# Hybrid encoder layer: token selection on two halves with a pairwise merge, group norm on token-major sums

## The reference

```
y = ys[0] + ys[1]
mean = jnp.mean(y, axis=-1, keepdims=True)
var = jnp.mean((y - mean) ** 2, axis=-1, keepdims=True)
y = ((y - mean) * lax.rsqrt(var + GN_EPS)).reshape(B, T, RWKV_WIDTH) * lnx_w + lnx_b
...
return ((y + bonus) * g).astype(z.dtype)
```

```
cap = CAPACITY_FACTOR * n // N_EXPERTS
aff = jax.nn.softmax((x @ w_router).astype(jnp.float32), axis=-1)
gates, idx = lax.top_k(aff.T, cap)
xe = x[idx]
```

## Time and profile before

| | us |
|---|---|
| median of 3 runs | 3022.91 (3021.03 to 3023.69) |
| the profiled execution | 3021.64, span 3019.8 |
| TensorE busy | 2716.5 (90%) |
| VectorE busy | 1978.3 (66%) |
| ScalarE busy | 1429.4 (47%) |
| GpSimd busy | 317.2 (11%) |
| mean granted TensorE clock | 0.947 of full speed |

### The profile page before, as it was taken

How to read it: one execution, slowest core, us unless ns; L and a number is a source line. 1 busy time by engine, 2 the same in 40 slices (tenths; PEclk the granted TensorE clock), 3 DMA queues, 4 the chain that set the end, 5 groups by cost and what they waited for, 6 DMA issues and landing times. The chain is left out here.

```text
span 3019.8 us, 89945 instructions
## 1 busy us (share of the span) xinstructions
PE 2716.5 (90%) x39070; PEld 2112.2 (70%) x39070; DVE 1978.3 (66%) x3171; ACT 1429.4 (47%) x2140; POOL 317.2 (11%) x260
## 2 busy tenths in 40 slices
PE   5999988987999999937917999999999999999994
PEld 3455544666999999924506777788887777788882
DVE  3344066875655655452278888888888888888882
ACT  3211156772222222231224666666666666666663
POOL 0000000002131131123100100000111000001000
PEclk8999998998999999978957999999999999999997
DMA  4114143003221121034207999999999999999984
GB/s 130 33 38 144 28 166 136 1 1 86 69 65 46 52 74 53 4 147 148 109 21 281 313 302 301 325 315 311 317 314 309 308 307 298 327 318 310 316 275 156
DMA packets 283336, 547.75 MB, mean 181 GB/s; under 512 B 13344, under 2 KB 96928, under 8 KB 283008
## 3 DMA queue, kind: packets, MB, share of 16 engines
q1 hardware_dynamic: 274160, 508.57, 49.2%
q0 software_dynamic: 8848, 34.08, 4.3%
HBM read 490.18 MB, written 52.43 MB: 180 GB/s over the span
## 5 line engine op out<-in xcount | busy, mean ns | idle before, releaser
L1658 DVE SCALAR_TENSOR_TENSOR arena<-arena 128x1024 f16<-128x1024 f32 x768 | 904.5, 1221 | 99.2 <-ACT arena L1603 98.9
L1558 PE MATMUL ps<-arena 128*128 128x160 f16 x12288 | 855.3, 233 | 4.2 <-DVE arena L1667 3.1
L1558 PEld LDWEIGHTS ps<-arena 128*128 128x128 f16 x12288 | 851.9, 98 | 7.7 <-DVE arena L1667 3.2
L1603 ACT ACTIVATE arena<-arena 128x1024 f16<-128x1024 f32 x768 | 766.7, 1050 | 150.6 <-PE ps L1583 149.3
L879 PE MATMUL ps<-arena 64*64 64x32 f32 (+2 forms) x14080 | 499.3, 224 | 22.4 <-DVEq L1044 21.3
L879 PEld LDWEIGHTS ps<-arena 64*64 64x64 f32 x14080 | 479.2, 135 | 27.9 <-DVEq L1044 21.5
L1575 PE MATMUL ps<-arena 128*128 128x512 f16 x1536 | 368.0, 392 | 0.0
L387 PE MATMUL ps<-arena 128*128 128x512 f16 (+1 forms) x1584 | 285.7, 344 | 0.7 <-ACT arena L236 0.7
L1575 PEld LDWEIGHTS ps<-arena 128*128 128x128 f16 x1536 | 143.3, 100 | 186.2 <-issue 41.8
L387 PEld LDWEIGHTS ps<-arena 128*128 128x128 f16 x1584 | 154.8, 98 | 131.9 <-ACT arena L236 1.2
L1624 ACT ACTIVATE arena<-ps 128x160 f32<-128x160 f32 x256 | 77.6, 303 | 253.1 <-PE ps L1558 252.9
(11 more groups left out here) (215 smaller groups left out, 2873.3 us busy)
## 6 DMA issues: line engine op xcount, KB each, us to landing
arena<-w_gate SPq DMA_DIRECT2D x128, 1024.0 KB, 5.7
arena<-w_up SPq DMA_DIRECT2D x128, 1024.0 KB, 6.0
arena<-w_down SPq DMA_DIRECT2D x128, 1024.0 KB, 7.0
arena<-feat SPq DMA_DIRECT2D x120, 256.0 KB, 4.7
feat<-arena SPq DMA_DIRECT2D x20, 640.0 KB, 3.0
arena<-w_in SPq DMA_DIRECT2D x21, 512.0 KB, 4.0
arena<-tokens SPq DMA_DIRECT2D x20, 512.0 KB, 3.9
feat<-arena POOLq DMA_DIRECT2D x1, 7680.0 KB, 22.8
```

The lines of the kernel that those rows point to most:

```text
L1558: ins = pe.matmul(ps[:, o:o + SLOTS], part(4 * c + 2 * w + k // 4, pw) [:, k % 4, f * P:(f + 1) * P], xT2[:, px, k], start=(k == 0 and i = ...
L1603: act.activation(split[k % SPLIT][:, q * PW:(q + 1) * PW], ring[k % RING][:, q * PW:(q + 1) * PW], ACT.Copy, scale=W_SCALE).then_inc(w_hi, 1)
L1658: v.scalar_tensor_tensor(split[k % SPLIT][:, WCH + q * PW:WCH + (q + 1) * PW], ring[k % RING][:, q * PW:(q + 1) * PW], W_SCALE, split[k % ...
```

## The change

In the group norm the sums of squares are formed with tokens on partitions: `token_var` multiplies the squares, as weights, with a two-column matrix of ones per head, so that one PSUM tile of 128x20 holds the sums of all 1280 tokens and two heads. Root and reciprocal work on these 20 columns. `spread` brings the result back to channels by products with the identity, whose weights are one column broadcast to 64. Each stage is done in place in `yacc`. The low halves of the output weights move from GpSimd to VectorE, as does the gate product of the last f, and ScalarE makes the high halves in one step. The output weights come in two transfers; the gain table, a new 128x128 matrix `flip` (the identity with reversed columns) and the router weights are loaded behind them.

```diff
         with nc.Block() as block:
             @block.sync
...
-                sp.dma_start(wo_raw, w_out.rearrange("(k p) n -> p k n", p=P)).then_inc(wo_in, 16)
-                sp.dma_start(wr, w_router.rearrange("(k p) n -> p k n", p=P)).then_inc(wo_in, 16)
-                sp.dma_start(g2n, gains[1:2, :].partition_broadcast(P)).then_inc(wo_in, 16)
+                for b in range(2):
+                    sp.dma_start(wo_raw[:, RT * b:RT * b + RT], w_out[RT * b * P:(RT * b + RT) * P]
+                                 .rearrange("(k p) n -> p k n", p=P)).then_inc(wo_in[b], 16)
                 for b in range(2):
                     sp.dma_start(x6[:, b], tokens[b * P:(b + 1) * P, :]).then_inc(x6_in[b], 16)
+                sp.dma_start(g2n, gains[1:2, :].partition_broadcast(P)).then_inc(tables_in, 16)
+                sp.dma_start(flip, c_mask[:, 2 * P + (4 + 2 * len(LEVELS)) * C:]).then_inc(tables_in, 16)
+                sp.dma_start(wr, w_router.rearrange("(k p) n -> p k n", p=P)).then_inc(tables_in, 16)
...
                 pool.wait_ge(post_in, 32)
-                for f in range(RT):
-                    for k in (2 * f, 2 * f + 1):
-                        pool.wait_ge(wo_hi, k + 1)
-                        pool.tensor_tensor(wo2[:, k, 1], wo_raw[:, k], wo2[:, k, 0], ALU.subtract).then_inc(wo_lo, 1)
+                for f in range(RT - 1):
                     pool.wait_ge(normed_ready, f + 1)
-                    pool.tensor_tensor(yacc[:, f], cen[:, f % 2], gate[:, f], ALU.mult).then_inc(post_done, 1)
+                    pool.tensor_tensor(yacc[:, f], yacc[:, f], gate[:, f], ALU.mult)
...
+                def head_sum(f):
                     if f:
                         pe.wait_ge(centred, f)
-                    head_sum(0, yacc[:, f]).then_inc(sum_psum, 1)
-                    pe.wait_ge(std_ready, 2 * f + 1)
-                    head_sum(1, csq[:, f % 2]).then_inc(var_psum, 1)
+                    for o, c in CHUNKS:
+                        ins = pe.matmul(ps[:, o:o + c], onesbd[:, :], yacc[:, f, o:o + c], start=True, stop=True)
+                    ins.then_inc(sum_psum, 1)
+
+                def token_var(f):
+                    pe.wait_ge(squared, f + 1)
+                    for t in range(NTT):
+                        o = (3 + 4 * (f % 2)) * 512 + 2 * t
+                        ins = pe.matmul(ps[:, o:o + 2], csq[:, f % 2, t * P:(t + 1) * P], head_col,
+                                        start=True, stop=True)
+                    ins.then_inc(var_psum, 1)
+
+                def spread(f):
+                    pe.wait_ge(rstd_ready, f + 1)
+                    if f:
+                        pe.wait_ge(normed_ready, f)
+                    for t in range(NTT):
+                        for h in range(2):
+                            ins = pe.matmul(ps[C * h:C * h + C, 2048 + t * P:2048 + (t + 1) * P],
+                                            rstd[:, f % 2, t, h:h + 1].broadcast_to([P, C]),
+                                            ident[:, :], start=True, stop=True)
+                    ins.then_inc(rstd_psum, 1)
+
+                head_sum(0)
+                head_sum(1)
+                token_var(0)
+                for f in range(RT):
+                    if f + 2 < RT:
+                        head_sum(f + 2)
+                    spread(f)
+                    if f + 1 < RT:
+                        token_var(f + 1)
...
+                def square(f):
                     act.wait_ge(centred, f + 1)
-                    act.activation(csq[:, f % 2], cen[:, f % 2], ACT.Square).then_inc(std_ready, 1)
+                    act.activation(csq[:, f % 2], yacc[:, f], ACT.Square).then_inc(squared, 1)
+
+                def root(f):
                     act.wait_ge(var_psum, f + 1)
                     if f >= 2:
-                        act.wait_ge(normed_ready, f - 1)
-                    act.activation(inv_s[:, f % 2], ps[:, 2048:2048 + NT], ACT.Sqrt, bias=cst[:, 1:2],
-                                   scale=1.0 / 64).then_inc(std_ready, 1)
-
...
+                        act.wait_ge(rstd_psum, f - 1)
+                    act.activation(rstd[:, f % 2].rearrange("p a b -> p (a b)"),
+                                   bank(3 + 4 * (f % 2), 2 * NTT), ACT.Sqrt, bias=cst[:, 1:2],
+                                   scale=1.0 / C).then_inc(std_ready, 1)
+
+                def weights_hi(first, end):
+                    act.wait_ge(wo_in[first // RT], 16)
+                    for k in range(first, end):
                         if k >= 2:
                             act.wait_ge(wo_lo, k - 1)
-                        act.copy(wo2[:, k, 0], wo_raw[:, k]).then_inc(wo_hi, 1)
+                        act.activation(wo2[:, k, 0], wo_raw[:, k], ACT.Copy, scale=W_SCALE).then_inc(wo_hi, 1)
...
-                    if f >= 2:
-                        v.wait_ge(post_done, f - 1)
-                    v.scalar_tensor_tensor(cen[:, f % 2], ps[:, 0:NT], -1.0 / 64, yacc[:, f],
+                    v.scalar_tensor_tensor(yacc[:, f], ps[:, 0:NT], -1.0 / C, yacc[:, f],
...
+                def invert(f):
+                    v.wait_ge(std_ready, f + 1)
+                    x = rstd[:, f % 2].rearrange("p a b -> p (a b)")
+                    v.reciprocal(x, x).then_inc(rstd_ready, 1)
+
+                def normed(f):
+                    y = yacc[:, f]
+                    v.wait_ge(rstd_psum, f + 1)
+                    v.scalar_tensor_tensor(y, y, pars[:, P_LW + f:P_LW + f + 1], ps[:, 2048:2048 + NT],
+                                           ALU.mult, ALU.mult)
+                    v.drain()
+                    if f == 0:
+                        v.wait_ge(post_in, 32)
+                    v.scalar_tensor_tensor(y, y, pars[:, P_LB + f:P_LB + f + 1], bonus[:, f],
+                                           ALU.add, ALU.add).then_inc(normed_ready, 1)
+
+                def weights_lo(first, end):
+                    for k in range(first, end):
+                        v.wait_ge(wo_hi, k + 1)
+                        v.scalar_tensor_tensor(wo2[:, k, 1], wo_raw[:, k], W_SCALE, wo2[:, k, 0],
+                                               ALU.mult, ALU.subtract).then_inc(wo_lo, 1)
...
                 centre(0)
-                v.wait_ge(post_in, 32)
-                for f in range(RT):
-                    if f + 1 < RT:
-                        centre(f + 1)
-                    v.wait_ge(std_ready, 2 * f + 2)
-                    v.reciprocal(inv_s[:, f % 2], inv_s[:, f % 2])
-                    v.drain()
-                    v.scalar_tensor_tensor(cen[:, f % 2], cen[:, f % 2], pars[:, P_LW + f:P_LW + f + 1],
-                                           inv_s[:, f % 2], ALU.mult, ALU.mult)
-                    v.drain()
-                    v.scalar_tensor_tensor(cen[:, f % 2], cen[:, f % 2], pars[:, P_LB + f:P_LB + f + 1],
-                                           bonus[:, f], ALU.add, ALU.add).then_inc(normed_ready, 1)
+                centre(1)
+                invert(0)
+                centre(2)
+                normed(0)
+                invert(1)
+                centre(3)
+                normed(1)
+                weights_lo(0, 2)
+                invert(2)
+                normed(2)
+                invert(3)
+                weights_lo(2, 4)
+                normed(3)
+                v.drain()
+                v.tensor_tensor(yacc[:, RT - 1], yacc[:, RT - 1], gate[:, RT - 1], ALU.mult)
+                weights_lo(4, KD)
```

```diff
                 for t in range(NTT):
-                    if t >= 2:
-                        pe.wait_ge(affT_read, t - 1)
-                    pe.transpose(ps[0:NE, (t % 2) * 512:(t % 2) * 512 + P], logit[:, t], ident[:, :]).then_inc(affT_psum, 1)
+                    rows = slice(32 * (t // 4), 32 * (t // 4) + NE)
+                    ins = pe.matmul(ps[rows, (t % 4) * P:(t % 4 + 1) * P], logit[:, t], ident[:, :],
+                                    start=True, stop=True)
+                    if t % 4 == 3 or t == NTT - 1:
+                        ins.then_inc(affT_psum, 1)
...
-                for t in range(NTT):
-                    act.wait_ge(affT_psum, t + 1)
-                    act.copy(aff[:, t * P:(t + 1) * P],
-                             ps[0:NE, (t % 2) * 512:(t % 2) * 512 + P]).then_inc(affT_read, 1)
+                for g, n in enumerate((HALF, HALF, T1)):
+                    act.wait_ge(affT_psum, g + 1)
+                    act.copy(aff[32 * g:32 * g + NE, 0:n], ps[32 * g:32 * g + NE, 0:n])
...
+                v.memset(aff, -1.0)
+                v.memset(first_row, 0.0)
+                v.drain()
+                v.memset(first_row[32:32 + NE], float(HALF))
+                v.memset(first_row[64:64 + NE], float(T0))
...
-                    pe.transpose(ps[:, n * 512:n * 512 + NE], src[:, 0:CAP0], ident[0:NE, 0:NE])
-                    ins = pe.transpose(ps[0:CAP1, n * 512 + NE:n * 512 + 2 * NE], src[:, CAP0:SLOTS],
```

(37 more changed lines are left out.)

71 lines of the change are left out of this document (41 added, 30 removed).

## The result

The changed kernel takes 2968.28 us (median of 4 runs, 2965.15 to 2971.12), the kernel before on the same chip 3023.3 (3021.03 to 3025.28): ratio 0.9818, 95% interval [0.9801, 0.9835]. The profiled execution took 2968.59 us, 53.1 under that of before.

What follows compares the result with a forecast made beforehand. VectorE's serial rounds bound selection; group norm, far from any engine's limit, spends 32.6 of VectorE's 50.6 us on four reciprocals. Selection -29.6, transposes +1.3, group norm -31.3 make -59.6: 3021.6 to 2962.0 us, 8-in-10 range 2949 to 2984.

Steps and rivals of the forecast that it cites:

- Selection: Stage of maximum, index and replacement rounds on VectorE: 31.1 us less in rounds, 1.5 more on the way out, net -29.6 us.
- The line through two row lengths: Selection rounds on 512-token rows, interpolated between 256 and 1024 tokens: 2.395 us a round, 1.53 for the last.
- The way out: Selection, from the cast to GpSimd's gather: 1.83 us before, forecast 1.5 us longer, bounds 0.8 and 4.
- Transposes: Routing probabilities between group norm and selection: 3.8 us before, 5.0 after, forecast +1.3 us, bounds -0.7 and +4.8.
- The pass with 16 weight columns: One of 20 TensorE passes transposing the routing probabilities, at the lower clock level: taken as 0.22 us.
- Group norm: Stage where the four wide reciprocals go: forecast 52.5 us long instead of 83.8, -31.3 us.
- wait 12: Group norm: VectorE's waits after the first normalized tile, mainly for the spread, taken as 12 us from 9 to 24.
- so 0.2 to 1.6 us; I leave it inside the 12: Group norm: cost of two GpSimd products beside two-SBUF-input VectorE operations, counted within VectorE's 12 us of waits.
- an overlap of 0.27 us: A normalization beside the end of a 2.12 us GpSimd operation: 1.36 us where its like takes 1.28.
- the 1.55 that I held against the rival: Length in us that the overlapped normalization would have had if GpSimd made VectorE wait wholly; argument against the rival.
- GpSimd's gate product stops VectorE outright: Group norm rival: weight halves behind two products each wait one out, 2 x 2.88 us, in all 2968; chance 0.10.
- The other rivals: TensorE's lower clock bounds group norm, 2980, 0.16; selection per-operation cost, 2987, 0.03; weight-load waits from 0.33 us a pass, 3033, 0.03.

## Why the prediction was right, and where it was wrong

**Selection,** -29.6 forecast, -28.7 measured. The line through two row lengths held: 2.420 us a round for 2.395, the last 1.59 for 1.53, and 80 partitions cost, by that line, no more than 16. The way out was under-sized: +2.0 for +1.5, inside its bounds.

**Transposes,** +1.3 forecast, -0.1 measured. The pass with 16 weight columns took 2.72/20 = 0.136 us at the granted clock of 0.50, not 0.22: what I held for the price of the upper level with 128 columns is the price of the lower with 16. (The sum in the forecast gives +1.2, not +1.3.)

**Group norm,** -31.3 forecast, -32.1 measured, but by two errors that cancel. The spread cost 0.06 us a pass as forecast (2.40 for 40). The first tile was normalized 18.5 us after the first sum, forecast 17.5. From there VectorE was to work 23.0 us and wait 12. It was busy 27.2 and waited 6.6 of the 33.8 us up to GpSimd's first cast in the next stage.

**The failed step** is "so 0.2 to 1.6 us; I leave it inside the 12", the price of GpSimd's products beside VectorE's operations. It was 5.4 us of VectorE's time, half of it on the stage; most of the rest stood where VectorE would have waited for the spread, so the two errors are not independent. I had read the price from an overlap of 0.27 us, in which the one had nearly ended when the other began: such a row can hardly tell a slower operation from one that stands until the other is done. The halves that stood ended 1.1 us behind the product's end, where one alone takes 1.22, so some 0.1 us of an overlap costs nothing. By that estimate the row should have shown about 1.4 us, not the 1.55 that I held against the rival; it showed 1.36. My rival "GpSimd's gate product stops VectorE outright" was right as a mechanism: two pairs, 2.7 us each for its 2.88. The rule that I named there, the Trainium skill, "SBUF — State Buffer", section "SBUF: two separate sides", holds here, and the row that I set against it was too short to speak against it. That the rival's 2968 is also the measured time is chance: the group norm ended where the forecast had it, since VectorE waited less than I took: TensorE was at its upper level until the 6.10 us pause, and the lengthened pairs filled some of its waits, which come to 9.0 us without the products.

**The rest.** From 2962.0 to the profiled 2968.6 are 6.6 us. The change's own stages gave 1.3 more than forecast; 4.6 came from the spread up to the norm, 5.3 from the experts, where TensorE's wait behind VectorE's code fetch is 3.9; the projection, the gap ahead of the first maximum and the final norm came out 2.5 shorter together than the forecast had them, and the execution lies 2.3 us above its span instead of 1.8. The other rivals fell: TensorE's clock bounded no round for long, and no pass came near 0.33 us (the worst spread 4.53/40 = 0.11).

## What to carry to other kernels

Before work is laid on GpSimd to spare VectorE, look at what VectorE runs beside it: where both take two operands from SBUF, the product cost VectorE almost its full length (2.7 of 2.9 us), and doing it on VectorE in 1.5 us was cheaper (group norm 46.3 for 48.2). Put the small operation that another engine waits for ahead of the long ones in the list: here that took the group norm from 52.4 to 48.2 us. That it keeps TensorE's clock up as well is not shown; the clock fell behind a pause of 1.15 us too. And when a stage that nobody touched is longer, take its spread over a few runs first, and then look for code packets and a wait without a releaser: empty instructions can move a fetch under a wait that is there anyway.

## What the runs showed that I had not expected

- Two low halves beside GpSimd's product: 4.80 to 5.04 us, 3.51 where the product began 1.6 us ahead, without it 2.29 to 2.35. The product itself takes 2.9 us when it starts at least 0.3 us ahead, 3.8 to 3.9 when VectorE starts ahead of it or within 0.03 us behind.
- A code fetch of VectorE just behind a loop: 3.3 to 5.9 us of standstill, at nearly one place of its instruction list, so that instructions put in ahead of the loop decide where in the last expert it falls.
- Same code up to the group norm, 1288.4 to 1295.6 us in thirteen profiles. That spread of 7.2 us is more than the gate product or the code fetch costs.
